# Two transformer layers and two hybrid layers on one core: masks staged earlier on GpSimd, weight slabs of the memory projection reordered, output projections begun in two parts

## The chip, the cores and the metric

The kernel runs on one core of a Trainium2 chip. Its time is the device time of one launch in microseconds, and of several launches the median is taken. TensorE (PE in the profile) multiplies, VectorE (DVE) and ScalarE (ACT) read and write both memories, GpSimd (POOL) works on SBUF alone, and SyncE (SP) issues all transfers. Every wait in the code is a semaphore wait written by hand.

## The reference, cut to what matters

There are 512 tokens of 1024 features (`x`), 256 memory tokens (`mem`), and four layers. All arithmetic is fp32 in and out.

```python
mem_n = rmsnorm(mem, norm_mem)
for i in range(2):                       # layers 0 and 1
    h = rmsnorm(x, norm_mix[i])
    mk, mv = split(mem_n @ w_mem_kv[i])  # 4 memory heads of 64
    q, k, v, qm = split(h @ w_in[i])     # 12 query heads
    y_tok = windowed_gqa(q, k, v, sink)  # layer 0: window, ALiBi, sink
          | neighbourhood_attn(q, k, v, rpb)  # layer 1: bias rpb[dr, dc], masked outside 16 columns
    y_mem = memory_attn(qm, mk, mv)
    x = x + concat(y_tok, y_mem) @ w_out[i]
    h = rmsnorm(x, norm_ffn[i])
    x = x + (silu(gate) * up) @ w_down[i]
x = rmsnorm(x, norm_final)
h = concat(meta_tokens, x)               # 16 + 512 tokens
# layer 2: conv branch and gated delta rule, then mix @ w_out, then a conv FFN
# layer 3: banded attention with 16 heads and 4 kv heads, then a conv FFN
```

## The kernel before

**Tiling.** Everything is held feature-major: a tile is 128 features by all tokens. Weights come in slabs: one slab is the weights of one output tile of 128 features, 8 blocks of 128 by 128 (512 KB), or 11 blocks for the down projections. There are 352 slabs in one fixed order. `raw` holds two of them, one in each of two slots (`s` is 0 or 1, `q` counts pairs of slabs).

**One slab's way.** SP loads it (`load_slabs`, L468; it waits for `lo_done`, that is for the split of the slab two before it, because it overwrites the same slot). ACT writes its rounded upper part `w_hi` (`split_hi`, L754, in two halves of four blocks; it waits until PE is through with the slab two before it). POOL writes the rest `w_lo = raw - w_hi` (`split_half`, L535, same halves). PE then does three products for each of the 8 blocks (`slab`, L1134: `w_hi` by `hi`, `w_hi` by `lo`, `w_lo` by `hi`), where `hi` and `lo` are the same split of the activations. `begin` (L1125) waits for the first half of `w_lo` and for the PSUM accumulator of slot `s` (`acc_free`), `second_half` (L1131) for the other half. Slot 0 accumulates in PSUM banks 0 and 1, slot 1 in banks 2 and 3.

**The start (`memkv`).** Eight slabs multiply the normed memory (256 columns). PE does slab 0, then `sum_squares` (L1150), which adds the squares of the memory up over the partitions, then slab 1, then slabs 2 to 7 (`first_pair`, L1160). ACT forms the root (`root_mean`) from it and DVE needs it to drain slab 0. For every slab ACT and DVE also round one tile of `x` for layer 0 (`round_tile`, `square`, `rest_of_tile`, `add_square`). SP issues slab 0, the vectors, the memory, slab 1, the constants, `x`, the meta tokens, three small rows, `w_ba`, the first ALiBi block (L500), and then slab 2 and the following (L471).

**Attention (`attend`).** A tile is two heads; for every tile PE, DVE, ACT and POOL go through its blocks of 128 queries (a pair in the code is one tile and one block). In PE's step of a pair stand its scores (L1250), the transposes of the probabilities two pairs back (L1263), and the product with the values three pairs back (L1280, L1284). DVE adds the bias to the scores and takes the maximum (`add_least`, L1558), ACT does the exponential (L861), moves the transposed probabilities (L873), and copies y (`move_y`, L892) and its upper part (`y_hi`, L897). POOL writes the lower part (`y_lo`, L637). The same POOL loop stages the tile that comes next, one chore in each of four blocks, each ahead of that block's `y_lo`:

```python
return [stage_q, stage_k, stage_v, mask]
```

`mask` (L612) works in layer 1 only: it writes `bias_sb = rpb_raw + grid_mask`, two instructions of 128x896, one for each head, and waits for the four transfers of `rpb_raw` (L508), which in turn wait until both masks of the tile before are written. DVE waits for both masks before the first block of a tile (L1703).

**Output projection (`out`).** Eight output tiles. It contracts over 8 activation tiles: the tiles of the attention outputs in layers 0, 1, 3; four tiles of the conv branch (`gated_lo`) and four of the delta heads (`head_lo`, L694) in layer 2. Before:

```python
if st.y2:
    pe.wait_ge(gated_lo, 4)
    pe.wait_ge(head_lo, 4)
else:
    pe.wait_ge(y_lo_ready, st.pair0)
many(st.slab0 // 2, DT // 2, st.blk, h_hi[st.h], h_lo[st.h])
```

In layers 0 and 1 it has one chunk of 512 columns, in layers 2 and 3 two of 264. In layer 2 it comes after `tile_norm` of the heads, in which PE only does the mean squares (L1373).

## Time and profile before

| what | value |
|---|---|
| median of 3 runs | 2661.07 us (2659.7 to 2661.27) |
| the profiled execution, its own time | 2662.7 us |
| its span in the profile | 2660.9 us |
| TensorE busy | 2564.9 us (96%) |
| VectorE, ScalarE, GpSimd busy | 922.4, 965.7, 1222.1 us (35, 36, 46%) |
| mean granted clock of TensorE | 0.985 |
| transfers | 212.91 MB, mean 80 GB/s |

The span runs from the first to the last instruction; the profiled execution's own time is 1.8 us longer. TensorE's records are counted busy from issue to a modelled end, so a gap between them is real idle time, and the granted clock tells at which of its two levels a stretch ran.

### The profile page before, as it was taken

The numbers are of one execution on the slowest core, as the hardware profiler recorded it, in microseconds if no ns is written. First come the engines' busy times: TensorE is split into PE (matmuls) and PEld (weight loads), VectorE is DVE, ScalarE is ACT, GpSimd is POOL, SyncE is SP. The second block draws the span as 40 slices with busy tenths as digits, with TensorE's granted clock in tenths as the row PEclk, the third lists the DMA queues.
The fourth block names the chain that finished last, engine by engine and source line by source line (L and its number), as shares of the span: only waits on it lengthen the run. The fifth ranks groups of instructions, "written<-read, shape, count | busy, mean of one in ns | idle before, by whom it ended". The sixth has DMA issues, their size and how long they took to land.

```text
span 2660.9 us, 46536 instructions
## 1 busy us (share of the span) xinstructions
PE 2564.9 (96%) x16181; PEld 2211.8 (83%) x16181; DVE 922.4 (35%) x1716; ACT 965.7 (36%) x2241; POOL 1222.1 (46%) x1032
## 2 busy tenths in 40 slices
PE   7999999999998999999998887999999999999999
PEld 6767888888866888888998787999999967998897
DVE  4253211222143321125653343441442254441341
ACT  4384222232276322224333223321233486332231
POOL 5454444444474544444342453444444354444443
PEclk9999999999998999999999898999999999999999
DMA  5212232232230223222221001222222201232222
GB/s 168 83 41 79 95 105 85 94 103 79 95 68 22 92 95 103 87 98 100 87 80 56 1 17 41 94 93 89 87 96 84 83 2 41 87 95 96 91 96 97
DMA packets 80487, 212.91 MB, mean 80 GB/s; under 512 B 30336, under 2 KB 33024, under 8 KB 80384
## 3 DMA queue, kind: packets, MB, share of 16 engines
q1 hardware_dynamic: 80384, 211.56, 25.0%
q8 instruction: 61, 1.00, 0.2%
q14 instruction: 42, 0.34, 0.0%
HBM read 209.44 MB, written 2.10 MB: 79 GB/s over the span
## 4 chain that ended last, share of the span: by engine, by line
PE 89%; issue 3%; ACT 3%; DVE 2%; POOL 2%; POOLq 0%; DMA 0%; DVEq 0%; ACTq 0%; SPq 0%
PE ps L1145 78%; PE ps L1381 3%; PE ps L1250 1%; PE ps L1263 1%; PE ps L1280 1%; ACT s_sb L861 1%; POOL w_lo L538 1%; ACT p_t L873 1%; DVE s_sb L1558 0%; PE ps L1284 0%; POOL bias_sb L620 0%; POOL h_lo L637 0%; PE ps L1199 0%; PE ps L1360 0%; PE ps L1154 0%
## 5 line engine op out<-in xcount | busy, mean ns | idle before, releaser
L538 POOL TENSOR_TENSOR w_lo<-raw,w_hi 128x512 fp32r<-128x512 f32 (+1 forms) x704 | 977.7, 1410 | 1181.9 <-ACT w_hi L762 1181.9
L762 ACT ACTIVATE w_hi<-raw 128x512 fp32r<-128x512 f32 (+1 forms) x704 | 426.5, 653 | 1366.7 <-PE ps L1145 1353.8
L1145 PE MATMUL ps<-h_hi,w_hi 128*128 128x264 f32 (+2 forms) x3216 | 903.8, 330 | 15.2 <-POOL h_lo L694 8.0
L1145 PE MATMUL ps<-h_lo,w_hi 128*128 128x264 f32 (+2 forms) x3216 | 897.4, 329 | 0.0
L1145 PE MATMUL ps<-h_hi,w_lo 128*128 128x264 f32 (+2 forms) x3216 | 896.1, 328 | 0.0
L1145 PEld LDWEIGHTS ps<-h_hi,w_hi 128*128 128x128 f32 x3216 | 543.1, 189 | 76.9 <-issue 18.1
L1145 PEld LDWEIGHTS ps<-h_lo,w_hi 128*128 128x128 f32 x3216 | 543.3, 189 | 57.4 <-issue 1.0
L1145 PEld LDWEIGHTS ps<-h_hi,w_lo 128*128 128x128 f32 x3216 | 541.9, 189 | 55.3
L1145 PE MATMUL ps<-act_hi,w_lo 128*128 128x512 f32 (+1 forms) x880 | 280.9, 352 | 0.0
L1145 PE MATMUL ps<-act_hi,w_hi 128*128 128x512 f32 (+1 forms) x880 | 280.3, 351 | 0.0
L1145 PE MATMUL ps<-act_lo,w_hi 128*128 128x512 f32 (+1 forms) x880 | 279.3, 350 | 0.0
L1533 DVE TENSOR_TENSOR x<-x,ps 128x512 f32<-128x512 f32 (+3 forms) x96 | 66.5, 693 | 443.7 <-PE ps L1145 443.7
L1145 PEld LDWEIGHTS ps<-act_lo,w_hi 128*128 128x128 f32 x880 | 153.7, 188 | 24.4
L1145 PEld LDWEIGHTS ps<-act_hi,w_lo 128*128 128x128 f32 x880 | 153.7, 188 | 24.3
L1145 PEld LDWEIGHTS ps<-act_hi,w_hi 128*128 128x128 f32 x880 | 153.9, 188 | 23.3
L1533 DVE TENSOR_TENSOR ps<-gated,ps 128x512 f32<-128x512 f32 (+1 forms) x88 | 61.6, 700 | 171.0 <-PE ps L1145 170.7
L1528 DVE SCALAR_TENSOR_TENSOR ps<-padded,vec,ps 128x528 f32<-128x528 f32 (+1 forms) x132 | 101.2, 767 | 25.1 <-issue 15.5
L861 ACT ACTIVATE s_sb<-s_sb,n_max 128x512 f32<-128x512 f32 (+5 forms) x176 | 97.4, 553 | 10.8 <-DVE n_max L1558 10.8
L637 POOL TENSOR_TENSOR h_lo<-y_sb,h_hi 128x128 fp32r<-128x128 f32 (+3 forms) x104 | 45.7, 440 | 120.5 <-ACT h_hi L897 119.7
L1263 PE MATMUL ps<-cst,s_sb 128*128 128x128 f32 (+1 forms) x568 | 92.7, 289 | 8.5 <-ACT s_sb L861 7.6
L1533 DVE TENSOR_TENSOR act_lo<-ps,act_hi 128x512 f32 (+1 forms) x88 | 61.2, 696 | 104.4 <-ACT act_hi L941 104.4
L1533 DVE TENSOR_TENSOR padded<-ps,rstd 128x528 f32<-128x528 f32 (+1 forms) x56 | 39.4, 703 | 154.2 <-PE ps L1145 143.9
(219 smaller groups left out, 2282.8 us busy)
## 6 DMA issues: line engine op xcount, KB each, us to landing
raw<-slabs_d SPq DMA_DIRECT2D x288, 512.0 KB, 3.5
raw<-slabs_d SPq DMA_DIRECT2D x64, 704.0 KB, 4.0
rpb_raw<-rpb_d SPq DMA_DIRECT2D x24, 224.0 KB, 4.1
bias_sb<-alibi_d SPq DMA_DIRECT2D x6, 384.0 KB, 3.8
x<-x_d SPq DMA_DIRECT2D x1, 2048.0 KB, 12.6
out_d<-x SPq DMA_DIRECT2D x8, 256.0 KB, 4.6
mem_in<-mem_d SPq DMA_DIRECT2D x1, 1024.0 KB, 8.5
dn_cst<-dn_consts_d SPq DMA_DIRECT2D x1, 512.0 KB, 4.8
```

The source lines that it names most:

```text
L538: nc.gpsimd.tensor_tensor(w_lo[:, s, a * P:b * P], raw[:, s, a * P:b * P], w_hi[:, s, a * P:b * P].bitcast(f32), ALU.subtract).then_inc(lo ...
L637: nc.gpsimd.tensor_tensor(h_lo[st.h][:, st.y + i, q], y_sb[st.h][:, (i * nb + b) % 2, 0:c["nq"]], h_hi[st.h][:, st.y + i, q].bitcast(f32), ...
L762: nc.scalar.activation(w_hi[:, s, a * P:b * P], raw[:, s, a * P:b * P], ACT.Copy)\
L861: nc.scalar.activation(s_h, src, ACT.Exp, bias=n_max[0:p.nq, p.slot, h:h + 1], scale=sign, accum_out=p_sum[0:p.nq, p.slot, h:h + 1]).then_ ...
L873: last = nc.scalar.activation(p_t[:, p.slot, h, 0:full, 0:p.nq], src[:, 0:full, 0:p.nq], ACT.Copy)
L1145: last = nc.tensor.matmul(ps[:, s * 2 * BANK + po:s * 2 * BANK + po + n], w[:, s, wk], a[:, k, to:to + n], start=(k == 0 and w is w_hi and ...
L1250: last = nc.tensor.matmul(bank(2 * p.slot + h)[0:p.nq, col:col + n], a[hp, p.tile_slot, p.q], b[hp, p.tile_slot, k0:k0 + n], start=(b is k ...
L1263: last = nc.tensor.transpose(bank(4 + h)[0:n, j * P:j * P + p.nq], s_sb[0:p.nq, p.slot, h, 1 + col:1 + col + n], ident[0:p.nq, 0:p.nq])
L1280: nc.tensor.matmul(out[HD * h:HD * h + HD, 0:p.nq], v_st[0:n, p.tile_slot, vb, HD * h:HD * h + HD], p_t[0:n, p.slot, h, j, 0:p.nq], start= ...
L1381: last = nc.tensor.matmul(out[:, h, :], lhs(h), rhs(h), start=True, stop=True)
L1528: return nc.vector.scalar_tensor_tensor(*a, **kw)
L1533: return nc.vector.tensor_tensor(*a, **kw)
```

## The change

1. **Masks.** In layer 1 POOL's chores for a tile become: queries; keys and the first head's mask; the second head's mask; values. DVE waits for the mask of each head ahead of that head's addition, no longer for both ahead of the tile.
2. **Start.** PE does slab 0, slab 1, and then the sum of squares. SP issues slab 2 right behind `x`, and slab 3 behind `w_ba`, ahead of the first ALiBi block. `x` gets a semaphore of its own (`x_loaded`), for which ACT waits; DVE waits for the small loads as before.
3. **Output projections.** The first pair of slabs is done in two parts: blocks 0 to 3 of slab 0 and of slab 1, then blocks 4 to 7 of slab 0 and of slab 1 (`project_out`). PE waits for each activation tile only ahead of its block. The other three pairs are done as before. The number of products is the same.

```diff
@@ -102,7 +102,8 @@
         up = norm(gain, blk)
-        add("out", blk=blk, y2=conv and layer == 0, post=up, to=1 - side[0])
+        add("out", blk=blk, y2=conv and layer == 0, post=up, to=1 - side[0],
+            n=len(out[-1].blocks) if out[-1].kind == "att" else None)
         slabs(DT, UP)
@@ -346,7 +347,7 @@
-        mem_loaded, cst_loaded, loaded = sem("mem_loaded"), sem("cst_loaded"), sem("loaded")
+        mem_loaded, cst_loaded, x_loaded, loaded = (sem(n) for n in ("mem_loaded", "cst_loaded", "x_loaded", "loaded"))
         raw_full = [sem(f"raw_full{s}") for s in range(RING)]
@@ -373,7 +374,7 @@
-        N_FIRST, N_LOADS = 2, 6
+        N_FIRST, N_LOADS = 2, 5
         META_T, SEQ_T = slice(0, META), slice(META, TOK)
@@ -458,19 +459,22 @@
             sp.dma_start(cst[:, :], d["consts"]).then_inc(cst_loaded, 16)
-            sp.dma_start(x[:, :, META:TOK], d["x"].rearrange("(m p) t -> p m t", p=P)).then_inc(loaded, 16)
+            sp.dma_start(x[:, :, META:TOK], d["x"].rearrange("(m p) t -> p m t", p=P)).then_inc(x_loaded, 16)
+
+            def load_slabs(q, s, size, src, at):
+
+                sp.wait_ge(lo_done, 2 * (2 * q + s - 1))
+                sp.dma_start(raw[:, s, 0:size * P], src[at]).then_inc(raw_full[s], 16)
+
+            load_slabs(1, 0, UP, d["slabs8"], 2)
             sp.dma_start(x[:, :, 0:META], d["meta"].rearrange("(m p) t -> p m t", p=P)).then_inc(loaded, 16)
-            def load_slabs(q, s, size, src, at):
-
-                sp.wait_ge(lo_done, 2 * (2 * q + s - 1))
-                sp.dma_start(raw[:, s, 0:size * P], src[at]).then_inc(raw_full[s], 16)
-
-            at, seen = RING, {UP: RING, DOWN: 0}
+            load_slabs(1, 1, UP, d["slabs8"], 3)
+            at, seen = 2 * RING, {UP: 2 * RING, DOWN: 0}
@@ -609,20 +613,26 @@
-                def mask(i):
-
-                    if st.bias != "rpb":
-                        return
-                    pool.wait_ge(rpb_full, i * 64 + 64)
-                    if not isinstance(i, int) or (i - 1) * nb + st.pair0 >= 1:
-                        pool.wait_ge(max_ready, 2 * ((i - 1) * nb + st.pair0))
-                    for h in range(2):
-                        nc.gpsimd.tensor_tensor(
-                            bias_sb[:, i % 2, h, :].rearrange("p (r c) -> p r c", c=GRID), rpb_raw[:, h, :, ::-1],
-                            grid_mask.unsqueeze(1).to_broadcast([P, RPB_R - 1, GRID]), ALU.add)\
-                            .then_inc(rpb_masked, 1)
-
-                return [stage_q, stage_k, stage_v, mask]
+                def mask(i, h):
+
+                    if h == 0:
+                        pool.wait_ge(rpb_full, i * 64 + 64)
+                        if not isinstance(i, int) or (i - 1) * nb + st.pair0 >= 1:
+                            pool.wait_ge(max_ready, 2 * ((i - 1) * nb + st.pair0))
+                    nc.gpsimd.tensor_tensor(
+                        bias_sb[:, i % 2, h, :].rearrange("p (r c) -> p r c", c=GRID), rpb_raw[:, h, :, ::-1],
+                        grid_mask.unsqueeze(1).to_broadcast([P, RPB_R - 1, GRID]), ALU.add).then_inc(rpb_masked, 1)
+
+                def k_and_mask(i):
+                    stage_k(i)
+                    mask(i, 0)
+
+                def second_mask(i):
+                    mask(i, 1)
+
+                if st.bias == "rpb":
+                    return [stage_q, k_and_mask, second_mask, stage_v]
+                return [stage_q, stage_k, stage_v]
@@ -645,16 +655,15 @@
                             pool.wait_ge(acc_free[s], (st.slab0 - 2) // 2)
-                    chores[0](0)
-                    chores[1](0)
-                    chores[3](0)
+                    for chore in chores[:-1]:
+                        chore(0)
                     pool.wait_ge(val_kept, st.val0)
-                    chores[2](0)
+                    chores[-1](0)
                     for b in range(nb):
-                        if b < 4 and chores:
+                        if chores and b < len(chores):
                             chores[b](tile0)
@@ -844,7 +853,7 @@
                         root_mean(st.pre)
-                        act.wait_ge(loaded, 16 * N_LOADS)
+                        act.wait_ge(x_loaded, 16)
                     round_tile(st.post, x, h_hi[st.h], k)
@@ -1139,13 +1148,38 @@
                         pe.wait_ge(made, at + k + 1)
-                    wk = slice(k * P, (k + 1) * P)
-                    for w, a in ((w_hi, hi), (w_hi, lo), (w_lo, hi)):
-                        for po, to, n in chunks(blk):
-                            last = nc.tensor.matmul(
-                                ps[:, s * 2 * BANK + po:s * 2 * BANK + po + n], w[:, s, wk], a[:, k, to:to + n],
-                                start=(k == 0 and w is w_hi and a is hi), stop=(k == nb - 1 and w is w_lo))
+                    last = products(k, s, blk, hi, lo, nb)
                 last.then_inc(pe_done, 1)
+
+            def products(k, s, blk, hi, lo, nb):
+                wk = slice(k * P, (k + 1) * P)
+                for w, a in ((w_hi, hi), (w_hi, lo), (w_lo, hi)):
+                    for po, to, n in chunks(blk):
+                        last = nc.tensor.matmul(
+                            ps[:, s * 2 * BANK + po:s * 2 * BANK + po + n], w[:, s, wk], a[:, k, to:to + n],
+                            start=(k == 0 and w is w_hi and a is hi), stop=(k == nb - 1 and w is w_lo))
+                return last
+
+            def project_out(st):
+
+                q0, hi, lo = st.slab0 // 2, h_hi[st.h], h_lo[st.h]
+                for half in range(2):
+                    for s in range(RING):
+                        if half == 0:
+                            begin(q0, s)
+                        else:
+                            second_half(q0, s)
+                        for k in range(4 * half, 4 * half + 4):
+                            if s == 0 and st.y2 and k < 4:
+                                pe.wait_ge(gated_lo, k + 1)
+                            elif s == 0 and st.y2:
+                                pe.wait_ge(head_lo, k - 3)
+                            elif s == 0:
+                                pe.wait_ge(y_lo_ready, st.pair0 - st.n * (7 - k))
+                            last = products(k, s, st.blk, hi, lo, UP)
+                        if half == 1:
+                            last.then_inc(pe_done, 1)
+                many(q0 + 1, DT // 2 - 1, st.blk, hi, lo)
@@ -1181,7 +1215,9 @@
                     if layer == 0:
-                        first_pair(st, 0, mem_hi, mem_lo)
+                        slab(q, 0, 0, mem_hi, mem_lo, made=h_ready, at=DT * st.pre.n)
+                        slab(q, 1, 0, mem_hi, mem_lo)
+                        sum_squares(st.pre)
                     else:
@@ -1484,12 +1520,7 @@
                 elif st.kind == "out":
-                    if st.y2:
-                        pe.wait_ge(gated_lo, 4)
-                        pe.wait_ge(head_lo, 4)
-                    else:
-                        pe.wait_ge(y_lo_ready, st.pair0)
-                    many(st.slab0 // 2, DT // 2, st.blk, h_hi[st.h], h_lo[st.h])
+                    project_out(st)
                 elif st.kind == "ffn":
@@ -1699,8 +1730,7 @@
                         wait(alibi_full, 16 * p.tile + 16)
-                    if p.b == 0 and st.bias == "rpb":
-                        wait(rpb_masked, 2 * p.tile + 2)
+
                     if st.bias is None:
@@ -1714,6 +1744,8 @@
                     for h in range(2):
+                        if p.b == 0 and st.bias == "rpb":
+                            wait(rpb_masked, 2 * p.tile + h + 1)
                         first = 3e38
```

## Rows read from the trace of the kernel before

**Rows 1.** The page: engines' busy time, share, instructions.
```profile
PE 2564.9 (96%) x16181; PEld 2211.8 (83%) x16181; DVE 922.4 (35%) x1716; ACT 965.7 (36%) x2241; POOL 1222.1 (46%) x1032
```

**Rows 2.** Waits of PE: releaser, us in total, times, longest.
```profile
PE ps L1145 <- POOL h_lo L637: 6.1, 3, 2.1
```

**Rows 3.** Waits of all engines, same columns.
```profile
DVE s_sb L1558 <- POOL bias_sb L620: 18.3, 4, 4.7
...
ACT w_hi L762 <- DMA raw<-slabs_d: 12.9, 7, 2.6
```

**Rows 4.** Timeline of POOL in layer 1: start, us, instruction, idle before.
```profile
755.11 1.29 POOL L568 TENSOR_TENSOR k_lo<-qk,k_hi  x1 [0.17 <-POOL k_hi L566]
757.11 0.46 POOL L637 TENSOR_TENSOR h_lo<-y_sb,h_hi 128x128 f32 x1 [0.71 <-ACT h_hi L897]
...
760.72 4.15 POOL L620 TENSOR_TENSOR bias_sb<-rpb_raw,cst 128x896 f32 x2
```

**Rows 5.** Timeline of PE, scores of three pairs following each other.
```profile
772.90 0.50 PE L1250 MATMUL ps<-k_hi,q_hi 64*128 64x512 f32 x2
...
776.11 0.50 PE L1250 MATMUL ps<-k_hi,q_hi 64*128 64x512 f32 x2
...
780.72 0.50 PE L1250 MATMUL ps<-k_hi,q_hi 64*128 64x512 f32 x2 [1.34 <-DVE n_max L1558]
```

**Rows 6.** Timeline of DVE, first addition of tile 2.
```profile
764.90 0.69 DVE L1558 CUSTOM_DVE_ANT_0 s_sb<-ps,bias_sb 128x512 f32<-128x512 f32 x1 [4.67 <-POOL bias_sb L620]
```

**Rows 7.** Timelines of SP and POOL: loads of the biases, masks of tile 1.
```profile
736.49 59.60 SPq L508 DMA_DIRECT2D rpb_raw<-rpb_d  x20
...
743.02 4.15 POOL L620 TENSOR_TENSOR bias_sb<-rpb_raw,cst 128x896 f32<-128x896 f32 x2 [1.61 <-DMA rpb_raw<-rpb_d]
```

**Rows 8.** Timelines of SP, ACT and PE at the start.
```profile
3.63 0.87 SPq L461 DMA_DIRECT2D x<-x_d  x1
...
18.34 47.62 SPq L471 DMA_DIRECT2D raw<-slabs_d  x12
...
17.66 2.95 ACT L782 ACTIVATE ps<-mem_in 128x256 f32<-128x256 f32 x6 [2.54 <-DVE sq_sum L1533]
23.17 1.15 ACT L762 ACTIVATE w_hi<-raw 128x512 fp32r<-128x512 f32 x2 [2.56 <-DMA raw<-slabs_d]
...
30.43 1.15 ACT L762 ACTIVATE w_hi<-raw 128x512 fp32r<-128x512 f32 x2 [0.63 <-PE ps L1145]
...
21.27 1.22 PE L1154 MATMUL ps<-sq_sum,cst 128*128 128x256 f32 x2 [3.48 <-DVE sq_sum L1533]
```

**Rows 9.** Issues of transfers: count, size, us to landing.
```profile
x<-x_d SPq DMA_DIRECT2D x1, 2048.0 KB, 12.6
```

**Rows 10.** Timeline of PE, layer 1's output projection.
```profile
850.44 0.77 PE L1145 MATMUL ps<-h_hi,w_hi 128*128 128x512 f32 x1 [2.13 <-POOL h_lo L637]
...
856.79 0.40 PE L1145 MATMUL ps<-h_hi,w_hi 128*128 128x512 f32 x1
857.02 0.40 PE L1145 MATMUL ps<-h_lo,w_hi 128*128 128x512 f32 x1
```

**Rows 11.** Timeline of PE, layer 2's mean squares and output projection.
```profile
1608.87 3.89 PE L1373 MATMUL ps<-sq,cst 128*128 128x264 f32 x8 [6.74 <-ACT sq L1033]
1620.79 0.78 PE L1145 MATMUL ps<-h_hi,w_hi 128*128 128x264 f32 x2 [8.04 <-POOL h_lo L694]
...
1624.74 0.41 PE L1145 MATMUL ps<-h_hi,w_hi 128*128 128x264 f32 x2
```

**Rows 12.** Windows: us; busy PE, PEld, DVE, ACT, POOL; granted clock; DMA share, GB/s.
```profile
202.00:206.00 4.00, 1.87 (x20) 1.20 (x17) 1.10 (x4) 1.92 (x8) 1.82 (x4) 1.00 0.44 131
...
850.00:854.00 4.00, 3.56 (x9) 2.85 (x10) 0.00 (x0) 0.00 (x0) 0.07 (x1) 0.50 0.02 4
```

**Rows 13.** Timelines of ACT and POOL behind layer 0's first output slab.
```profile
211.58 1.15 ACT L762 ACTIVATE w_hi<-raw 128x512 fp32r<-128x512 f32 x2 [6.81 <-PE ps L1145]
...
212.29 3.00 POOL L538 TENSOR_TENSOR w_lo<-raw,w_hi 128x512 fp32r<-128x512 f32 x2 [6.99 <-ACT w_hi L762]
```

## The prediction

> **What bounds the kernel now.** I read the page first: TensorE is busy 2564.9 of 2660.9 us [rows 1], so the kernel is PE's own queue of work, and an edit counts only if it fills one of PE's gaps or changes its clock. Then PE's waits, and the waits of all engines for what stands behind them [rows 2, 3]. Three places belong to the change: three gaps before output projections, 6.1 us together, that end with the lower part of the last attention tile [rows 2], and one of 8.04 us in layer 2 that ends with the lower part of the last head [rows 11]; four waits of DVE for masks, 18.3 us, of which PE feels a part [rows 3, 5, 6]; and the start, where PE waits 3.48 us for the sum of squares and ACT waits 2.56 us for slab 2 [rows 8]. The timelines around each place tell who is late.
>
> **Masks.** POOL ends the keys of tile 2 at 755.11 + 1.29 = 756.40, writes a y_lo at 757.11, later another, and only then both masks, 760.72 to 764.87 [rows 4]. DVE could have gone on at 764.90 - 4.67 = 760.23 [rows 6]. PE feels it less, because work of earlier pairs is still queued: scores follow each other every 776.11 - 772.90 = 3.21 us, and across the stall in 780.72 - 776.11 = 4.61 us [rows 5]. One stall costs 1.40 us, and rows 3 count four of them: 5.6 us.
> After the change the first mask (4.15 / 2 = 2.1 us) runs from 756.4 to 758.5. The y_lo due at 757.11 follows until 759.0, then the second mask until 761.1. DVE wants the first at 760.2 and the second one addition (0.69 us, some 0.8 with its reading [rows 6]) later, at about 761.1. So the first is in time by 1.7 us and the second just so; a lateness of 0.2 us vanishes behind PE, which tolerated 3.3 of the 4.7 us before. What is late next: the y_lo of block 2 by 1.9 us and that of block 3 by about 1 us. Both free a slot of y that ACT refills one step (3.21 us) after the upper part that released them, so they fit. The values' copy moves behind them and is read by PE three steps after the tile's first scores, so it is covered by about 9 us. The bias loads: SP issues them when both masks of a tile are done (736.49) and they are there at 743.02, 6.5 us later [rows 7]. In steady state the second mask ends at 761.1 and the next first mask is due at 756.4 + 4 x 3.21 = 769.2, 8.1 us later; 1.6 us to spare. Tile 1 waits at 743.02 as before, with its values now behind its masks, which nobody needs yet. Without all this cover the term falls to 0; nothing can raise it over 5.6. I take **5.6**, bounds 3 to 5.6.
>
> **Output projections.** Nothing is removed but waiting. In layers 0, 1 and 3 the first parts of both slabs need tiles 0 to 3, ready long before. They are 24 products. A product of 512 columns takes 857.02 - 856.79 = 0.23 us [rows 10], so they take 5.6 us, and the last tile, only 2.1 us late at most [rows 2], is asked for after them. The 6.1 us go whole. In layer 2 PE ends the mean squares at 1608.87 + 3.89 = 1612.76 and starts the projection at 1620.79 [rows 11]. Now it starts at 1612.8. Two chunks of 264 columns take 0.24 us by the same rate, so 24 products plus three blocks of the second part (9 products) bring it to 1612.8 + 8.0 = 1620.8 at full clock, when the last head is there. It goes whole too, 8.0 us; the bound below is 7.5. I take 0.1 us off at each of the four hand-overs for the semaphores in front: **13.8**, bounds 12.5 to 14.1.
> What it makes late: slab 0 is now done at three quarters of the pair, so slab 2 of the stage must be split within one half-slab, 12 x 0.23 = 2.8 us. Before, ACT begins 0.1 us behind PE and POOL begins 0.7 us behind ACT (212.29 against 211.58), and its two halves take 3.00 us [rows 13]. The first half is there after 0.8 + 1.5 = 2.3 us, 0.5 us in time; the second after 3.8, wanted at 5.6. If that cover were gone, by a first half of 2.1 us, each stage would lose 0.1 to 0.3 us. The Trainium skill (GPSIMD Engine Reference, Specifications) says that GpSimd contends for its SBUF interface with VectorE's instructions that have two SBUF inputs, and DVE now does one of these in that stretch; this trace's row with such company is the 3.00 us for two halves, and by the rule a first half could only be longer than that, which costs under 1 us in all.
>
> **Clock.** In layer 1 the projection starts at half clock (0.50 in 850 to 854 [rows 12]): 15 products lie between 850.44 and 856.79 [rows 10], 6.35 us instead of 3.5, a loss of 2.85 us behind a gap of 2.13 us. Layer 0 had the same gap (PE busy 1.87 of 4 us) and kept 1.00 [rows 12], so this stretch is near the edge, and dense products in place of the gap should keep it above: **2.9**, bounds 0 to 2.9. In layer 2, 9 products between 1620.79 and 1624.74 take 3.95 us instead of 2.2: 1.8 lost [rows 11]. PE is already at half clock at 1608.87 (8 matmuls in 3.89 us, where a chunk at full clock takes half of 0.24), but then idles 8 us. Now it stays busy from there, so the rise comes earlier in the projection; all of the loss can go or none, and as the dense work now begins 4 us further back I take two thirds: **1.2**, bounds 0 to 1.8.
> The Trainium skill (TensorE: Matmul & The Clock Gate, What's actually happening) says that the fast level is granted after sustained activity and lost after idleness, and that the moment varies between runs of one kernel. By that rule the start of layer 1's projection may fall either way from run to run; this trace shows one of each for the same gap, and it is the second rival below.
>
> **Start.** PE's 24 products of slab 1 (256 columns, half of 0.23 us each, 2.8 us) fit the 3.48 us before the sum of squares, which itself stays at 21.27, since DVE's additions set it [rows 8]. Slab 2 is issued behind x, as soon as slab 0 is split; x lands at 3.63 + 12.6 = 16.2 [rows 8, 9], and slab 2 took 23.17 - 18.34 = 4.8 us from issue to its use, so it is there by 21.0 at the latest; ACT is free for it at 17.66 + 2.95 = 20.61. Its split moves up by 2.2 to 2.6 us, and the load of slab 4 with it. The root then waits for the sum (22.5), no longer for slab 2's split (24.3): 1.8 us earlier. PE's slab 2, which ended at 30.4 (ACT's wait [rows 8]), needs the root (two ACT operations of 2.95 / 6 = 0.5 us) and a drain by DVE, an estimated 1.4 us behind 22.5, then 2.8 us at full clock or 5.6 at half: end 26.7 to 29.5, so 0.9 to 3.7 us earlier. From there every split waits for its load, and every load for the split two before (seven waits, 12.9 us [rows 3]), so the chain carries the smaller of these gains to the first projection. I take **2.3**, bounds 0.9 to 3.0. Slab 3, the small loads and the ALiBi block have PE's and ACT's work until 24 us as cover; each moved issue costs SP under 1 us [rows 8].
>
> **The sum.** 5.6 + 13.8 + 2.9 + 1.2 + 2.3 = 25.8 us. Against the profiled execution's own time: 2662.7 - 25.8 = 2636.9. The median of the runs is 1.6 us below that execution, so **2635.3 us**.
>
> **The rivals.**
> *Likeliest*, all terms: 2633 to 2638; chance 0.52.
> *Layer 1's projection still starts at half clock*, or loses as much elsewhere: for it, that the sparse stretch in front of the gap stays as it is; against it, layer 0. 2635.3 + 2.9 = 2638.2; chance 0.2.
> *POOL becomes the mask's new delay*: second mask or bias load late in every tile, the 5.6 us stay: for it, only about 0 and 1.6 us of slack; against it, PE's 3.3 us tolerance. 2640.9; chance 0.07.
> *The start is hidden anyway*: SP is held up by the queue, slab 3 or `w_ba` comes late and ACT or DVE wait in place of slab 2. 2637.6; chance 0.08.
> *More than the sum*: a half-clock stretch of the memory attention goes too, worth about another 4 us. 2631; chance 0.07.
> *Slower*: the first pairs are written out instead of looped, 288 matmuls in four stages. If fetching code held PE, (25.8 + 5.3) / 288 = 0.11 us each would turn the result; against it, the first pairs of every other stage are written out already, and PE idles only 96 us in all [rows 1]. 2667 and more; chance 0.02.
> The remaining 0.04 lie between, half of it within 0.2% of before.
>
> **How the numbers follow.** A change under 0.2% (5.3 us) cannot be told from none here. All cases but the last two end faster: 0.94 faster with what lies between, 0.03 same, 0.03 slower. The range takes in the cases from more than the sum to POOL's delay: 2629.5 to 2642; about 0.1 is left out.
>
> **What the profile after would show.** Right: no wait of DVE for `bias_sb` beyond tile 1, scores every 3.21 us throughout; no wait of PE for `h_lo` at the four projections; 1.00 in the windows of layer 1's projection; slab 2's split at 20.6 to 21.0 and the first projection about 2.3 us earlier. Wrong: waits of PE for `w_lo` in the second pair of a projection, a wait of ACT for `y_lo` in layer 1, waits for `rpb_raw` in every tile, or a new half-clock stretch that gives back more than 3 us.

## The result and the profile after

The changed kernel takes 2638.09 us (median of 4 runs, 2631.97 to 2639.17), the kernel before 2661.17 us (median of 4, 2659.70 to 2662.09): a ratio of 0.9907, 95% interval 0.9893 to 0.9922, or 23 us. The forecast was 2635.3 us within 2629.5 to 2642.0. The profiled execution of the changed kernel is its shortest one, 2631.97 us with a span of 2630.1.

The page first, engines' busy time, to be held against [rows 1]:

```profile
PE 2553.7 (97%) x16181; PEld 2203.4 (84%) x16181; DVE 928.4 (35%) x1716; ACT 965.9 (37%) x2241; POOL 1218.4 (46%) x1032
```

PE does the same 16181 matmuls. Its span is 30.8 us shorter and its busy time 11.2 us: the first is gaps and clock together, the second, with the work the same, is mostly the clock's (a gap that is filled also takes the modelled end of the matmul before it out of the busy time).

Three of the waits of PE, in whose list the line for `h_lo` [rows 2] is gone:

```profile
PE ps L1286 <- ACT s_sb L870: 9.9, 10, 1.9
...
PE ps L1158 <- POOL w_lo L542: 1.7, 2, 1.1
...
PE ps L1158 <- DVE mk L1564: 1.6, 1, 1.6
```

Both waits for `w_lo` lie in the memory projection (34.1 and 41.2 us), none in an output projection. DVE's wait for `bias_sb`, 18.3 us in [rows 3], is gone from the list of all waits too. In layer 1, the timeline of POOL for one tile, and the scores of PE in the same stretch:

```profile
750.82 2.10 POOL L622 TENSOR_TENSOR bias_sb<-rpb_raw,cst 128x896 f32 x1
752.88 0.47 POOL L647 TENSOR_TENSOR h_lo<-y_sb,h_hi 128x128 f32 x1
753.29 2.11 POOL L622 TENSOR_TENSOR bias_sb<-rpb_raw,cst 128x896 f32 x1
```

```profile
756.36 0.50 PE L1286 MATMUL ps<-k_hi,q_hi 64*128 64x512 f32 x2
759.56 0.50 PE L1286 MATMUL ps<-k_hi,q_hi 64*128 64x512 f32 x2
762.76 0.50 PE L1286 MATMUL ps<-k_hi,q_hi 64*128 64x512 f32 x2
```

Two masks, with a `y_lo` between them, and scores every 3.20 us. The timeline before has the step of 4.61 us of [rows 5] four times in layer 1, that of the kernel after nowhere. Layer 1's output projection, timeline of PE and its window (columns as in [rows 12]), for [rows 10, 12]:

```profile
834.59 0.33 PE L1320 MATMUL ps<-cst,p_rec 128*128 128x128 f32 x1
834.68 0.48 PE L1158 MATMUL ps<-h_hi,w_hi 128*128 128x512 f32 x1
834.99 0.40 PE L1158 MATMUL ps<-h_lo,w_hi 128*128 128x512 f32 x1
```

```profile
834.00:838.00 4.00, 4.00 (x24) 3.22 (x24) 1.06 (x3) 1.30 (x6) 1.37 (x3) 1.00 0.39 131
```

The first product follows 0.09 us behind the start of the attention's last transpose, and a product takes 0.23 us, the rate of 2.4 GHz. Layer 2, timeline of PE for [rows 11]:

```profile
1589.33 3.89 PE L1409 MATMUL ps<-sq,cst 128*128 128x264 f32 x8 [6.75 <-ACT sq L1042]
1592.64 1.02 PE L1158 MATMUL ps<-h_hi,w_hi 128*128 128x264 f32 x2
...
1594.78 0.61 PE L1158 MATMUL ps<-h_lo,w_hi 128*128 128x264 f32 x2
1595.21 0.41 PE L1158 MATMUL ps<-h_hi,w_lo 128*128 128x264 f32 x2
...
1596.21 0.40 PE L1158 MATMUL ps<-h_hi,w_hi 128*128 128x264 f32 x2
```

From the second mean squares to the projection it was 1620.79 - 1608.87 = 11.92 us [rows 11] and is 1592.64 - 1589.33 = 3.31. The first five products still take 0.43 us and more, those behind 0.25. The start, timelines of ACT and PE for [rows 8]:

```profile
20.54 1.13 ACT L771 ACTIVATE w_hi<-raw 128x512 fp32r<-128x512 f32 x2
22.00 0.47 ACT L829 ACTIVATE rstd<-ps,vec 128x256 f32<-128x256 f32 x1 [0.33 <-PE ps L1188]
```

```profile
21.26 0.70 PE L1188 MATMUL ps<-sq_sum,cst 128*128 128x256 f32 x2
23.53 0.36 PE L1158 MATMUL ps<-mem_hi,w_hi 128*128 128x256 f32 x1 [1.57 <-DVE mk L1564]
```

ACT splits slab 2 at 20.54 instead of 23.17, at the early end of the forecast (20.6 to 21.0).

The split of slab 2 in layer 0's output projection, timelines of POOL and DVE, for [rows 13]:

```profile
209.37 3.01 POOL L542 TENSOR_TENSOR w_lo<-raw,w_hi 128x512 fp32r<-128x512 f32 x2 [7.43 <-ACT w_hi L771]
```

```profile
210.46 0.76 DVE L1559 SCALAR_TENSOR_TENSOR h_lo<-x,vec,h_hi 128x512 fp32r<-128x512 f32 x1 [1.17 <-ACT h_hi L778]
```

The two halves take as long as before (3.00 us).

### The profile page after: what moved, and what is told of

Same layout as the page of the kernel before. It is cut to its first block, busy times and chain, and to the rows that moved or that the text cites. A ratio compares the mean times of both kernels' runs of the same rounds, so it can differ in the third digit from the quotient of the medians.

```text
span 2630.1 us, 46507 instructions
## 1 busy us (share of the span) xinstructions
PE 2553.7 (97%) x16181; PEld 2203.4 (84%) x16181; DVE 928.4 (35%) x1716; ACT 965.9 (37%) x2241; POOL 1218.4 (46%) x1032
## 4 chain that ended last, share of the span: by engine, by line
PE 90%; ACT 3%; issue 3%; DVE 1%; POOL 1%; POOLq 0%; DMA 0%; ACTq 0%; DVEq 0%; SPq 0%
PE ps L1158 79%; PE ps L1417 3%; PE ps L1316 2%; PE ps L1299 2%; PE ps L1286 2%; ACT s_sb L870 1%; POOL w_lo L542 1%; ACT p_t L882 0%; PE ps L1320 0%; PE ps L1235 0%; PE ps L1396 0%; PE ps L1188 0%; PE ps L1458 0%; PE ps L1409 0%; POOL h_lo L647 0%
```

## The experiments

The tables below set the profiles side by side by stages of PE, from its timeline: S, from the start to layer 0's first attention scores; M, layer 1's attention up to its output projection; F, from there to the first down projection of layer 1. "Half" is the time of the stage at the lower of the two clock levels, twice the stretch times (1 - granted clock), summed over windows of some 8 us.

| profile | S | M (half) | F (half) |
|---|---|---|---|
| before | 119.6 | 113.31 (14.2) | 171.49 (6.0) |
| after | 116.2 | 103.08 (3.4) | 168.39 (0) |
| after, again | 118.6 | 103.07 (3.4) | 168.72 (0) |
| masks only | 121.0 | 107.78 (13.8) | 168.72 (0) |
| output projections only | 117.6 | 112.26 (20.5) | 168.72 (0) |
| start only | 118.8 | 114.68 (20.5) | 170.28 (3.4) |

**The whole change again, and its three parts one by one.** Each part alone is the hunks of the diff that belong to it, on the kernel before.

`r1_after_again`, the changed kernel unaltered:

> The changed kernel once more, nothing edited, to see how its time is spread and where a second profile of it finds TensorE at half clock. Theory M (the change gains what PE's gaps lose, 3.5 at the start, 5.6 at the masks, 14.7 at the projections, 23.8 us together, and the clock only spreads it): median 2635 to 2640, ratio 0.990 to 0.992, and a profile near 2637 shows the memory attention or the start of a projection at half clock where the profile at 2632 did not. Theory C (filled gaps also keep the clock up, for good): median nearer 2632, ratio 0.989, and no second profile with half clock at a projection's start in layers 0, 1 or 3.

`r2_masks_only`:

```diff
-                return [stage_q, stage_k, stage_v, mask]
...
+                    return [stage_q, k_and_mask, second_mask, stage_v]
...
-                        wait(rpb_masked, 2 * p.tile + 2)
...
+                            wait(rpb_masked, 2 * p.tile + h + 1)
```

> Of the change only the masks' part. Prediction's step: 5.6 us faster (ratio 0.998), scores every 3.21 us through all four tile changes, no wait of DVE for the masks past tile 1. Rival (POOL is the new delay): DVE still waits 1 to 3 us in each tile and PE regains less than 3 us. Clock: nothing here should change the stretch of layer 1's projection, which stays at half clock if the fall comes from the gap of 2.1 us in front of it.

`r3_outs_only`:

```diff
-                    many(st.slab0 // 2, DT // 2, st.blk, h_hi[st.h], h_lo[st.h])
+                    project_out(st)
```

> Of the change only the projections' part. Theory M: 14.7 us faster (ratio 0.9945), 2.1, 2.1, 1.9 and 8.6 us in the profile at the four projections. Theory C: about 18 us (ratio 0.993), because layer 1's projection no longer starts at half clock. Rival (slab 2 of the stage is split too late behind the interleaved pair): PE waits for w_lo 0.1 to 0.5 us in each of the four stages and the gain is 13 or less.

`r4_start_only`:

```diff
-                        first_pair(st, 0, mem_hi, mem_lo)
+                        slab(q, 0, 0, mem_hi, mem_lo, made=h_ready, at=DT * st.pre.n)
+                        slab(q, 1, 0, mem_hi, mem_lo)
+                        sum_squares(st.pre)
...
+            load_slabs(1, 0, UP, d["slabs8"], 2)
...
+            load_slabs(1, 1, UP, d["slabs8"], 3)
```

> Of the change only the start, both the PE order and the SP order. Prediction's term was 2.3 us, the profile of the whole change shows the first projection 3.5 us earlier; so 3.5 us faster (ratio 0.9987), and granted clock 1.00 from 12 us on. If the 3.5 us need anything of the other two parts (they do not touch this stretch): less.

| kernel | median (range), runs | ratio, 95% interval | gain of medians |
|---|---|---|---|
| before | 2664.42 (2659.50 to 2668.19), 23 | | |
| after, again | 2634.50 (2634.06 to 2642.59), 5 | 0.9896, 0.9881 to 0.9911 | 29.9 |
| masks only | 2657.86 (2653.21 to 2664.72), 12 | 0.9977, 0.9967 to 0.9987 | 6.6 |
| output projections only | 2642.30 (2641.76 to 2648.55), 5 | 0.9921, 0.9907 to 0.9934 | 22.1 |
| start only | 2662.20 (2658.33 to 2665.93), 11 | 0.9993, 0.9984 to 1.0002 | 2.2 |

The parts add up: 6.6 + 22.1 + 2.2 = 30.9 against 29.9. Of these gains the start's alone is not clear of noise: its interval reaches 1.0002.

Against what was expected: the changed kernel again has its median, 2634.50, between the two theories (2635 to 2640, and 2632), and its profile has half clock in S, at neither of the places that theory M named. Masks only gained what was expected, but layer 1's projection did not stay at half clock. Output projections only gained 22.1 us, more than either theory has (14.7 and some 18; at equal half clock, in the fit below, it is 16.3, between them); the rival's 13 is out. Start only was to gain 3.5 us with full clock from 12 us on; it gained 2.2 us by the medians, and its profile has 6.8 us at half clock in S.

The masks are worth 113.31 - 107.78 = 5.53 us in M at an equal amount of half clock, which is four times 4.61 - 3.20 = 1.41 us. For the gap ahead of a projection masks only is the plain witness, since it still has it; timeline and windows of PE:

```profile
844.51 0.33 PE L1289 MATMUL ps<-cst,p_rec 128*128 128x128 f32 x1
846.97 0.47 PE L1150 MATMUL ps<-h_hi,w_hi 128*128 128x512 f32 x1 [2.13 <-POOL h_lo L643]
```

```profile
843.00:847.00 4.00, 1.87 (x21) 1.17 (x19) 1.35 (x4) 2.22 (x10) 1.82 (x4) 1.00 0.45 131
847.00:851.00 4.00, 4.00 (x17) 3.25 (x18) 0.00 (x0) 0.00 (x0) 0.00 (x0) 1.00 0.01 4
```

Two things stand here. From start to start there are 2.46 us, in the kernel after 0.09: the gap is worth 2.37 us, more than the 2.13 of the idle column, since that counts from a modelled end and the next matmul can start ahead of it. And the projection runs at full clock behind this same gap, where before it ran at 0.50 [rows 12]. F says the same: 168.72 with the gap, 171.49 before. Each of these is read from one profile.

**Parts of the parts.** `r5_masks_swap`: both masks whole, in one chore behind the keys, ahead of the values; DVE waits for both as before.

```diff
-                return [stage_q, stage_k, stage_v, mask]
+                if st.bias == "rpb":
+                    return [stage_q, stage_k, mask, stage_v]
+                return [stage_q, stage_k, stage_v]
```

> The kernel before with one edit: the chore that writes both masks changes places with the values' copy; both masks stay in one chore, and DVE waits for both ahead of the tile as before. By the trace the second mask then ends 3.2 us sooner, at the equivalent of 761.7, and DVE, ready at 760.2, still waits 1.3 to 1.5 us in each of four tiles. Theory T (PE has about 3.3 us of queued work to live on): PE's stall of 1.34 us is gone all the same, and the kernel gains what the masks' part gained, 5 to 6.6 us (ratio 0.9977). Rival (the split by heads is what does it): a stall of 0.5 us or more stays in PE's rows and the gain is under 4 us.

`r6_outs_whole`: output projections only, with slab 0 whole and then slab 1 whole, but still a wait for each activation tile (the edit is shown against output projections only).

```diff
-                for half in range(2):
-                    for s in range(RING):
+                for s in range(RING):
+                    for half in range(2):
```

> The projections' part without its two parts: PE waits for each activation tile ahead of its block, but slab 0 is done whole and then slab 1. In layers 0, 1 and 3 the last tile is asked for after 21 products (4.9 us), late by 2.1 at most, so the 6.1 us go as with two parts. In layer 2 the last head comes 8.2 us after PE starts and 21 products take 5.1 us, 1.4 more for the half clock: PE waits 1.5 to 2 us more than with two parts. Expected 1.5 to 2 us slower than the projections' part in full, ratio 0.9925 to 0.993, and one wait of PE for the last head of that size. Rival (per-block waits alone give nothing, as slab 0 then holds slab 1 up): gain under 10 us.

`r7_start_pe`: PE's order at the start alone (the hunk with `sum_squares(st.pre)`).

> Only PE's order at the start: slab 1 ahead of the sum of squares; SP as before. Slab 2 still comes to ACT at 23.2, the root behind it, so PE idles some 3.7 us between the sum and slab 2 in place of 3.5 ahead of the sum. Expected: the gap only moves; first projection within 1 us of before, ratio 0.999 to 1.001.

`r8_start_sp`: SP's order and ACT's wait for `x_loaded` alone.

> Only SP's order at the start: slab 2 behind x, slab 3 ahead of the ALiBi block; PE does the sum before slab 1 as before. ACT has slab 2 split by 21.8 and the root by 23, but PE is in slab 1 at half clock until 27.4 and starts slab 2 there as before, and ACT's next splits wait for PE. Expected: 0 to 1 us. If this alone gives the 1.6 to 3.5 us of the start's part, the transfer was the bound and PE's order does nothing.

| kernel | median (range), runs | ratio, 95% interval |
|---|---|---|
| before | 2661.37 (2658.94 to 2665.58), 27 | |
| masks swapped, whole | 2656.48 (2652.25 to 2659.37), 11 | 0.9980, 0.9971 to 0.9989 |
| outputs, slabs whole | 2645.85 (2641.83 to 2648.39), 5 | 0.9935, 0.9922 to 0.9949 |
| start, PE alone | 2660.88 (2659.10 to 2667.18), 11 | 1.0001, 0.9992 to 1.0010 |
| start, SP alone | 2662.09 (2658.78 to 2665.49), 11 | 1.0001, 0.9992 to 1.0010 |

*Masks.* With whole masks DVE is late again, and PE does not feel it. Timelines of POOL, DVE and PE:

```profile
758.03 4.16 POOL L620 TENSOR_TENSOR bias_sb<-rpb_raw,cst 128x896 f32 x2
```

```profile
762.23 0.69 DVE L1559 CUSTOM_DVE_ANT_0 s_sb<-ps,bias_sb 128x512 f32<-128x512 f32 x1 [1.47 <-POOL bias_sb L620]
```

```profile
759.20 0.49 PE L1251 MATMUL ps<-k_hi,q_hi 64*128 64x512 f32 x2
762.40 0.50 PE L1251 MATMUL ps<-k_hi,q_hi 64*128 64x512 f32 x2
765.60 0.50 PE L1251 MATMUL ps<-k_hi,q_hi 64*128 64x512 f32 x2
```

The stall of DVE fell from 4.7 to 1.5 us, and scores keep their 3.20 us. The gain comes from the order; the split by heads adds nothing that the intervals show (0.9977 and 0.9980).

*Outputs.* With slabs whole PE runs into the wait for the last head of layer 2, and pays twice. Timeline of PE:

```profile
1611.38 0.41 PE L1150 MATMUL ps<-h_hi,w_lo 128*128 128x264 f32 x2
1613.41 0.51 PE L1150 MATMUL ps<-h_hi,w_hi 128*128 128x264 f32 x2 [1.61 <-POOL h_lo L695]
...
1614.24 0.64 PE L1150 MATMUL ps<-h_hi,w_hi 128*128 128x264 f32 x2
```

Just behind the gap the products go from 0.24 to 0.44 us each, until 1617.3. From the projection to layer 3's attention it takes 519.71 us against 515.92 with two parts: 3.8 us. From start to start the gap is worth 1613.41 - 1611.38 - 0.24 = 1.8 of them, and the slower products behind it some 1.7. The medians, 2645.85 and 2642.30, stand beside different runs of the kernel before, and the two intervals overlap; the difference is read from the traces. In the attention layers whole slabs wait for nothing either (waits of PE for `h_lo` of tiles: none), so the two parts are needed in layer 2 alone. It was expected to be 1.5 to 2 us slower than with two parts; the gap is of that size, and the clock behind it was not in that sum.

*Start.* Each half of it only moves the wait, as expected, and neither gains (1.0001 both). Timeline of PE with its order alone, then of ACT in the same kernel:

```profile
20.86 0.70 PE L1154 MATMUL ps<-sq_sum,cst 128*128 128x256 f32 x2 [0.59 <-DVE sq_sum L1535]
24.32 0.55 PE L1145 MATMUL ps<-mem_hi,w_hi 128*128 128x256 f32 x1 [2.77 <-DVE mk L1535]
```

```profile
21.77 1.15 ACT L762 ACTIVATE w_hi<-raw 128x512 fp32r<-128x512 f32 x2 [1.57 <-DMA raw<-slabs_d]
22.82 0.45 ACT L820 ACTIVATE rstd<-ps,vec 128x256 f32<-128x256 f32 x1
```

ACT waits for slab 2 and takes the root behind it, so DVE drains slab 0 late. With SP's order alone ACT splits slab 2 at 20.23, but the sum of squares still follows a wait of 3.48 us and slab 1 comes behind it.

**Where the clock comes in, and a better kernel.** In the profile after, what is left in the memory attentions of layers 0 and 1 are two gaps at their beginning, with the steps behind them at half clock. `r9_hold_clock` fills them with matmuls whose result nobody reads; output and other work are the same.

```diff
+                def step_and_fill(p):
+                    step(p)
+                    if st.bias is None and p.pos == 1:
+                        constants(4, 4, 256)
+                    if st.bias is None and p.pos == 2:
+                        pe.wait_ge(y_ready, st.pair0 - 1)
+                        constants(6, 3, 256)
...
-                    over_pairs(pe.Fori, st, step)
+                    over_pairs(pe.Fori, st, step_and_fill)
```

`constants(to, n, cols)` does n matmuls of `cols` columns into PSUM bank `to`, with constants on both sides.

> The kernel after the change with seven idle matmuls of 256 columns in each memory attention of layers 0 and 1: four behind the second step, three behind the third, where the profile after shows PE idle for 1.94 and 1.24 us (layer 0). Theory A (the half-clock steps are there because of these gaps, and PE's own work sets the length of the steps): the stretches at half clock of 6.9 us in layer 0's and 3.4 us in layer 1's memory attention go, the two or three steps in them fall from 3.44 us to 2.65 us each, and the kernel gains 1.6 to 4 us: 2633.5 to 2636.5 against 2638.1 for the change alone. Theory B (the steps wait for ACT's exponentials anyway): the clock is 1.00 there and the time stays within 1 us. Theory C: the idle matmuls are late in the queue and push the scores back: 1 to 3 us slower.

`r10_early_heads` begins layer 2's projection between the two mean squares:

```diff
-                    with pe.Fori(0, n // 2) as i:
+                    for i in range(2):
+                        if i == 1:
+                            part(out, 0, 0, 4)
...
+                part(out, 1, 0, 4)
+                part(out, 0, 4, 6)
+                part(out, 1, 4, 6)
+                part(out, 0, 6, 8)
+                part(out, 1, 6, 8)
```

Here `part(out, s, a, b)` does blocks a to b - 1 of slab s, with the waits of `project_out`.

> The kernel after the change, with layer 2's projection begun further ahead: blocks 0 to 3 of its first slab stand between the two rounds of mean squares of the heads (PE is idle there for 6.75 us), then blocks 0 to 3 of the second slab, blocks 4 and 5 of both, blocks 6 and 7 of both. Theory A (the last head, ready 8.3 us behind the second mean squares, now sets the end of the pair; slab 2's split begins late, behind slab 0's last block): the pair ends 1 to 3 us earlier, 2635 to 2637. Theory B (the work in the gap also ends the half clock behind it): the second mean squares take 2 us in place of 3.9 and the time falls by a further 1 to 2 us only if the heads follow. Rival: slab 2's split, now free only 0.7 us before it is wanted, gives all of it back: a wait of PE for w_lo of 1.5 us or more and no gain.

`r11_hold_early` has both edits:

> Both edits of the two kernels before this one together. If they are independent, the gains add: some 3 to 6 us under the change alone, about 2633.

`r12_no_start` is the change without its start (masks and output projections on the kernel before):

> The masks and the output projections of the change, with the start as before. If the start's term holds on top of the other parts as it does alone (2.2 us in medians, 1.6 us at an equal amount of half clock), this kernel is 1.5 to 2.3 us slower than the whole change: 2639.6 to 2640.4. Rival: the start only trades idle time for half clock, and this kernel is within 0.7 us of the whole change.

| kernel | median (range), runs | ratio, 95% interval |
|---|---|---|
| before | 2662.66 (2659.92 to 2665.32), 7 | |
| after, gaps filled | 2632.46 (2629.55 to 2634.60), 4 | 0.9890, 0.9873 to 0.9906 |
| after, early heads | 2636.15 (2633.86 to 2639.56), 4 | 0.9905, 0.9888 to 0.9922 |
| after, both | 2632.04 (2628.69 to 2633.42), 4 | 0.9881, 0.9865 to 0.9898 |
| after without the start | 2637.54 (2636.53 to 2641.98), 4 | 0.9910, 0.9894 to 0.9927 |

*Gaps filled.* First the kernel after, scores of the memory attention of layer 0 and windows over them, then the kernel with the gaps filled, its timeline and the same windows:

```profile
178.63 0.56 PE L1286 MATMUL ps<-k_hi,q_hi 64*128 64x256 f32 x2 [1.94 <-ACT s_sb L870]
...
181.90 0.58 PE L1286 MATMUL ps<-k_hi,q_hi 64*128 64x256 f32 x2 [1.24 <-ACT s_sb L870]
...
185.34 0.45 PE L1286 MATMUL ps<-k_hi,q_hi 64*128 64x256 f32 x2
```

```profile
179.00:183.00 4.00, 2.77 (x17) 1.92 (x16) 0.91 (x3) 1.77 (x7) 1.84 (x4) 0.50 0.00 0
183.00:187.00 4.00, 4.00 (x31) 2.78 (x31) 1.84 (x4) 2.60 (x10) 0.00 (x0) 0.69 0.00 0
```

```profile
176.88 1.99 PE L1332 MATMUL ps<-cst 128*128 128x256 f32 x8
178.88 0.39 PE L1286 MATMUL ps<-k_hi,q_hi 64*128 64x256 f32 x2
...
181.53 0.39 PE L1286 MATMUL ps<-k_hi,q_hi 64*128 64x256 f32 x2
...
184.27 0.39 PE L1286 MATMUL ps<-k_hi,q_hi 64*128 64x256 f32 x2 [0.68 <-ACT s_sb L870]
```

```profile
179.00:183.00 4.00, 3.86 (x32) 2.92 (x34) 1.72 (x4) 2.21 (x9) 2.11 (x4) 1.00 0.00 0
183.00:187.00 4.00, 2.72 (x28) 1.72 (x24) 1.25 (x4) 3.19 (x15) 0.00 (x0) 1.00 0.00 0
```

Steps of 3.27 and 3.44 us become 2.65 and 2.74. No stretch at half clock is left in either attention; layer 0's stage falls from 83.75 to 82.28 us, layer 1's from 103.08 to 102.51. The four and three matmuls stand as 8 and 6 records, and the scores follow at 178.88, where the others have ended (176.88 + 1.99 = 178.87). The trace shows theory A's mechanism. By its two ratios the change would take 2635 to 2638 us beside these runs, so the gain is 2.5 to 5.5 us; over all runs the mean span falls from 2634.8 to 2630.4. The interval (0.9873 to 0.9906) overlaps both of the change's, and in the profile the two stages give 2.0 us. The plainest pair is in this very set: early heads with and without the same fill, 2632.04 against 2636.15 us, mean spans 2629.8 and 2634.6.

*Early heads.* The work moved, and little came of it. Timeline of PE:

```profile
1593.01 3.88 PE L1424 MATMUL ps<-sq,cst 128*128 128x264 f32 x8 [3.82 <-ACT sq L1042]
...
1604.58 0.51 PE L1158 MATMUL ps<-h_hi,w_hi 128*128 128x264 f32 x2 [0.47 <-POOL h_lo L703]
...
1607.72 0.52 PE L1158 MATMUL ps<-h_hi,w_hi 128*128 128x264 f32 x2 [0.67 <-POOL w_lo L542]
```

Part of the work in the gap leaves 3.82 us of it, and the mean squares behind still run at half clock (3.88 us): theory B fails. The last head and then slab 2's split set the pace, as theory A has it. From the first mean squares to layer 3's attention it takes 526.8 us in place of 528.3 (8.80 + 3.31 + 516.22), a gain of 1.5 us, which the medians do not resolve from nothing. Both edits together are the best kernel of the study by the medians, but not clearly: its interval just overlaps that of the change in the first comparison (0.9893 to 0.9922) and widely that of the repetition (0.9881 to 0.9911). Against the fill alone the early heads add 0.4 us.

*Without the start.* This kernel was to take 2639.6 to 2640.4 us if the start's term holds on top of the rest. It takes 2637.54, its ratio is 0.9910 against 0.9907 and 0.9896 for the whole change, and that is what the rival said (within 0.7 us). A gain of the start on top of the other parts is not shown by these medians.

**All runs in one fit.** The granted clock of a run differs between executions of one kernel, and its time with it. I fitted by least squares the spans of the 148 runs for which span and clock are on record (those of the kernel before in the first comparison are not): a constant for each kernel and one slope for the time at half clock, 2 x span x (1 - mean clock). The slope is 0.215 us for each us at half clock (standard error 0.012). That is an average. Where PE is dense, as in layer 1's projection, the price is half a microsecond (3.1 us in F for 6.0). Why the average is lower is not shown: in the profile before PE is idle in only 23 of some 83 us at half clock. 44 of these 83, and 19 of the 23, lie in two stretches of layer 2, from 1450.5 and 1607.5 us on, where matmuls wait for other engines between each other.

| kernel (runs) | mean us at half clock | gain at equal half clock (standard error) |
|---|---|---|
| before (57) | 83.8 | 0 |
| after (9) | 66.8 | 22.4 (0.6) |
| masks only (12) | 87.7 | 5.6 (0.5) |
| masks swapped (11) | 78.2 | 5.2 (0.5) |
| output projections only (5) | 75.1 | 16.3 (0.7) |
| outputs, slabs whole (5) | 64.5 | 12.7 (0.7) |
| start only (11) | 92.4 | 1.7 (0.5) |
| start, PE / SP alone (11 each) | 75.9 / 83.2 | -1.0 / 0.2 (0.5) |
| after without the start (4) | 69.9 | 21.3 (0.8) |
| after, early heads (4) | 68.5 | 23.0 (0.8) |
| after, gaps filled (4) | 43.4 | 21.7 (0.9) |
| after, both (4) | 43.4 | 22.4 (0.9) |

The change's mean span is 26.1 us below before's (2634.8 against 2660.9): 22.4 of its own and 17 x 0.215 = 3.7 from the clock. The three parts give 5.6 + 16.3 + 1.7 = 23.6 one by one, within the errors of 22.4. Filling the gaps gives nothing of its own (21.7) and 23.4 x 0.215 = 5.0 by the clock. The runs come from four sets; with one more constant for each set the slope is 0.226 and no gain moves by more than 1.4 us.

## Why the prediction was right, point by point

The forecast of 25.8 us stands against 23 us in the first comparison, 29.9 in the second, and 26.1 over the mean of all runs. The main terms, masks and output projections, came true by their mechanism. That the total came so close is also luck: an output term that was too small and a stretch of the memory attention that was not in the sum stand against start and layer 2's clock, which were too large.

- **Masks, 5.6 (bounds 3 to 5.6).** 5.53 us in the stage, 5.6 in the fit. All four late steps are gone. The argument that the second mask was "just so" in time asked for more than is needed: 1.5 us of lateness cost nothing.
- **Output projections, 13.8 (12.5 to 14.1).** The mechanism was right and the term too small: 16.3 in the fit. Between masks only and the change without the start, which have the same half clock there, the stages ahead of the three projections fall by 86.75 - 84.42 = 2.33, 107.78 - 105.28 = 2.50 and 99.52 - 97.25 = 2.27 us: 7.1, not 6.1 less 0.3, because the idle column counts from a modelled end; layer 2 gave 11.92 - 3.31 = 8.61, not 7.9. Together 15.7, beyond the bound of 14.1. (14.1 less four times 0.1 is also 13.7 and not 13.8.) What stands with the profile before, "a gap between them is real idle time", is thus too simple: the idle column is short by the modelled end. The hand-over to slab 2 of the stage costs PE no wait, as forecast. The sum took the 3.00 us of its split as two equal halves. They are 1.30 and 1.75 us: in the profile after, 43 of the halves of 128x512 take some 1.75 us in place of 1.30, and 38 of these lie beside VectorE's `h_lo`, which reads two SBUF inputs. So the contention that the prediction reckoned with is in the trace, with 0.45 us as its price for POOL, but in layer 0 it falls on the second half, which has time. At the start it can fall on VectorE: beside two halves that take 2.70 us together (from 27.84 us) `h_lo` takes 1.55 us in place of 0.76 (from 29.53).
- **Slower by code fetch of the written-out pairs.** Nothing of it: in layers 0, 1 and 3 products follow each other at 0.23 and 0.24 us from the second on, in layer 2 from the sixth, behind half clock.
- **Clock in layer 1's projection, 2.9.** The size came true in this pair of profiles (171.49 to 168.39 us, 3.1); the three of the start, with 170.26 to 170.28, give 1.9. The reason, "dense products in place of the gap should keep it above", is not shown. All eight profiles in which the gap is filled have full clock there. But so have masks only and masks swapped, which keep the gap; the other four that keep it (before, and the three of the start) are at half in part. So a gap of 2.13 us is not enough to bring the fall, masks and output projections each go with full clock, and the whole change, which has both, can't tell them apart. In the profile before the fall comes inside the gap (granted clock 0.97 in 846 to 850). What decides it is open.
- **Clock in layer 2, 1.2 (0 to 1.8).** The first nine products take 1596.21 - 1592.64 = 3.57 us in place of 3.95: 0.4. Gap and clock together, from the second mean squares to the tenth product, it is 1624.74 - 1608.87 = 15.87 us before and 1596.21 - 1589.33 = 6.88 after: 9.0, where the sum had 7.9 + 1.2 = 9.1.
- **More than the sum.** Part of this rival happened beside the likeliest case: in layer 1's memory attention the half clock fell from 14.2 to 3.4 us, worth 105.28 - 103.08 = 2.2 us by the profile without the start, which has 13.8. It varies: in the profile with early heads that stage has 6.7 and 103.70.
- **Start, 2.3 (0.9 to 3.0).** Not resolved. It is 2.2 us in the medians alone, with an interval that includes no change, 1.7 (0.5) in the fit, and on top of the rest 1.1 (0.9) in the fit and nothing in the first comparison's median (2638.09 against 2637.54); layer 0's first scores come at 118.1 us in the mean of six profiles with it, at 119.6 in six without. The profile of the change shows 3.5 us, since it stayed at full clock from 24 us on; the repeated one did not, and shows 1.0. Windows of the kernel after, then of the same kernel again:

```profile
24.00:28.00 4.00, 4.00 (x34) 3.82 (x33) 3.56 (x6) 3.07 (x7) 3.10 (x3) 1.00 0.41 135
```

```profile
24.00:28.00 4.00, 4.00 (x23) 4.00 (x23) 3.58 (x5) 2.07 (x4) 2.91 (x2) 0.57 0.40 131
```

34 matmuls in 4 us in one execution, 23 in the other, of one kernel. That is what one profile can't tell: a term of 2 us that sits ahead of such a stretch is read from several. The Trainium skill (TensorE: Matmul & The Clock Gate, What's actually happening) says that the moment of the rise varies between runs of one kernel. The first rise agrees: products of 256 columns go from 0.21 to 0.12 us each at 18.3 us in the first profile and at 17.3 in the second. The two windows show a fall that one execution has and the other has not. One thing here reads wrong at first: the granted clock of 12 to 16 us stands as 1.00 in both profiles, though every product in it takes 0.21 us, as at half clock. Ahead of its first recorded change this column misleads, and the time from product to product must be looked at.
- **The chances.** The five cases that end faster make 0.94 without what lies between, and of the cases only the last is slower, not the last two; the split into faster, same and slower is off by 0.02. It changes nothing in the forecast.

## What to carry to other kernels

Where one engine is busy nearly all the time, list its gaps, and price each from start to start, not by its idle column; add what the clock behind it does, and take that part from several executions. A late operand is cheapest to hide by doing first what doesn't need it, but look which consumer really feels the lateness: here masks 1.5 us late cost nothing, and whole slabs did as well as halves in three of four stages. Two edits that hand the wait to each other (a sum and a load behind it) must be tried together, and judged together; here even the two together are worth some 1 to 2 us, which a handful of runs doesn't show. And a term that comes true in size has not had its reason shown: look whether a kernel without that reason shows it too.

## What the runs showed that I had not expected

- The same gap of 2.13 us ahead of layer 1's projection is followed by granted clock 0.50 in one kernel and 1.00 in another that differs only before it (one profile each; masks swapped shows 1.00 behind its gap too).
- A gap of 1.6 us in the middle of dense products, as the slabs-whole kernel has, was followed by seven products at 0.44 us each in place of 0.24, and the stage took 3.8 us more.
- Seven idle matmuls of 256 columns in each of two memory attentions, in time that PE would have waited, went with a mean span 4.4 us shorter (4.8 between the two kernels with early heads), by the fit all of it the clock's (43 us at half clock in place of 67).
